# Down matrices 2 to 24 in one 4 MB load each, the last chunks of experts 0 and 1 one by one, and a residual sum moved behind the first up product

## What is computed

```python
x = x + merged @ W_out
h2 = rmsnorm(x, norm_ffn_g)
# per token: the best 4 of 32 router logits, softmax over these four
for e in range(32):                      # rows xb: the tokens that chose e
    gu = xb @ w_gu[e] + b_gu[e]          # (1024, 2048): "up", 8 MB
    g = minimum(gu[:, :1024], 7); lin = clip(gu[:, 1024:], -7, 7)
    y = ((lin + 1) * g * sigmoid(1.702 * g)) @ w_down[e] + b_down[e]   # (1024, 1024): "down", 4 MB
    x[tokens] += weight * y
out = rmsnorm(x, norm_final_g)
```

## Time and profile before

| | us |
|---|---|
| median of 3 runs | 1184.96 (1184.89 to 1185.57) |
| the profiled execution | 1184.24 |
| its span, first to last instruction | 1182.4 |

### The profile page before, as it was taken

One profiled execution on the slowest core, in us unless ns is written; L12 is line 12 of the kernel. 1 busy time (PEld: TensorE's weight loads), 2 busy tenths in 40 slices (PEclk: granted clock), 3 DMA queues, 4 the chain that ended last, 5 costly groups with the idle time before them and its releaser, 6 DMA issues.

```text
span 1182.4 us, 14724 instructions
## 1 busy us (share of the span) xinstructions
PE 1103.6 (93%) x6066; PEld 582.5 (49%) x6066; DVE 391.4 (33%) x647; ACT 247.5 (21%) x389; POOL 4.5 (0%) x10
## 2 busy tenths in 40 slices
PE   8999999999999989898898989898999989998996
PEld 8999999983443333333333333333344333433332
DVE  6768655563222322222222222222222222222212
ACT  6444773432111111111111111111111111111113
POOL 0000000000000000000000000000000000000000
PEclk9999999999999999999999999999999999999999
DMA  9955744689999999999999999999999999999996
GB/s 332 319 175 184 270 164 158 257 318 409 428 425 427 431 431 430 431 427 436 431 430 430 432 432 427 433 430 431 429 432 431 428 432 425 433 428 432 411 422 264
DMA packets 61131, 452.13 MB, mean 382 GB/s; under 512 B 3570, under 2 KB 34535, under 8 KB 40871
## 3 DMA queue, kind: packets, MB, share of 16 engines
q1 hardware_dynamic: 60272, 449.53, 92.0%
q0 software_dynamic: 560, 1.74, 0.5%
q10 hardware_dynamic: 263, 0.34, 0.1%
HBM read 450.53 MB, written 1.06 MB: 382 GB/s over the span
## 4 chain that ended last, share of the span: by engine, by line
DMA 49%; PE 47%; SPq 1%; DVE 1%; ACT 1%; issue 1%; DVEq 0%
DMA dring<-in_w_down_dram 41%; PE bank L1175 17%; PE bank L1546 13%; PE bank L1495 10%; DMA ring<-in_w_gu_dram 7%; PE bank L1440 1%; DMA ring<-in_w_mem_kv_dram 1%; PE bank L1385 1%; PE bank L1266 0%; PE bank L1415 0%; PE bank L1507 0%; PE bank L1449 0%; SPq L315 0%; ACT w_high L487 0%; PE bank L1612 0%
## 5 line engine op out<-in xcount | busy, mean ns | idle before, releaser
L1495 PE MATMUL bank<-ring,region_x 128*64 128x512 f32 x2048 | 456.2, 597 | 6.9 <-DMA ring<-in_w_gu_dram 6.9
L1546 PE MATMUL bank<-dring,region_r 128*64 128x512 f32 x1024 | 247.4, 634 | 56.2 <-DMA dring<-in_w_down_dram 55.7
L1495 PEld LDWEIGHTS bank<-ring,region_x 128*64 128x64 f32 x2048 | 141.0, 137 | 279.7 <-issue 264.8
L1546 PEld LDWEIGHTS bank<-dring,region_r 128*64 128x64 f32 x1024 | 74.4, 145 | 226.2 <-issue 135.0
L1175 PE MATMUL bank<-hT_high,w_high 128*128 128x256 f32 x384 | 109.9, 286 | 0.7 <-DVE hT_low L747 0.7
L1175 PE MATMUL bank<-hT_high,w_low 128*128 128x256 f32 x384 | 108.6, 283 | 0.0
L1175 PE MATMUL bank<-hT_low,w_high 128*128 128x256 f32 x384 | 108.6, 283 | 0.0
L755 DVE TENSOR_TENSOR w_low<-ring,w_high 128x2048 fp32r<-128x2048 f32 x39 | 89.3, 2289 | 52.5 <-ACT w_high L487 52.4
L1083 DVE TENSOR_SCALAR region_r<-bank 128x512 f32<-128x512 f32 x32 | 22.1, 692 | 244.9 <-PE bank L1495 244.9
L1102 DVE SCALAR_TENSOR_TENSOR y_parts<-bank,region_r,y_parts 64x512 fp32r<-64x512 f32 x31 | 23.1, 744 | 215.1 <-ACT y_parts L656 215.1
L639 ACT ACTIVATE region_r<-region_r 128x512 f32<-128x512 f32 x32 | 20.1, 630 | 315.0 <-DVE region_r L1083 315.0
(11 more groups left out here) (248 smaller groups left out, 872.1 us busy)
## 6 DMA issues: line engine op xcount, KB each, us to landing
ring<-in_w_gu_dram SPq DMA_DIRECT2D x50, 4096.0 KB, 25.7
dring<-in_w_down_dram SPq DMA_DIRECT2D x58, 2048.0 KB, 24.2
ring<-in_w_gu_dram SPq DMA_DIRECT2D x17, 2048.0 KB, 12.6
ring<-in_w_in_dram SPq DMA_DIRECT2D x26, 1024.0 KB, 6.4
ring<-in_w_gu_dram SPq DMA_DIRECT2D x22, 1024.0 KB, 8.8
dring<-in_w_down_dram SPq DMA_DIRECT2D x11, 1024.0 KB, 11.6
ring<-in_w_out_dram SPq DMA_DIRECT2D x4, 1024.0 KB, 4.9
ring<-in_w_mem_kv_dram SPq DMA_DIRECT2D x3, 1024.0 KB, 11.8
```

Source lines behind the costliest of these rows:

```text
L1495: last = mm(ps[64 * half:64 * half + 64, :], xg[u // 2][:, c, 64 * (u % 2):64 * (u % 2) + 64], ring[:, slot0 + c, k * F + half * 512:k * F ...
L1546: last = mm(ps[64 * half:64 * half + 64, :], lhsT, dring[:, c // 2, at:at + 512], start=(c == 0), stop=(c == KC - 1))
```

## The change

Six things are changed.

1. `down_slots` reads the matrix as `(p k) n` with k = 8: each partition holds eight neighbouring rows, and n slots of it are one run of n x 8 KB. The runs of loads of every expert stand in two tables, `UP_RUNS` and `DOWN_RUNS`. Down matrices 2 to 24 are one load of 4 MB; before, they were two of 2 MB. Matrices 1 and 25 to 29 stay in two loads, 0, 30 and 31 in four (the last slot of 31 in two). SyncE waits for all slots that a load fills.
2. `down` waits once, at c = 0, for a matrix that comes in one load.
3. The hidden values must stand in the order of the rows: VectorE's reordering goes by eight where it went by four, and four transposes of 128 x 128 become 16 products of 64 x 64 blocks with a piece of the identity.
4. In the small products the slots are transposed first, then the hidden values.
5. Chunks 6 and 7 of experts 0 and 1 are four loads of 1 MB: chunk 6 of both experts after mixer piece 38 of 40, chunk 7 of both after piece 39. Before, they were two loads of 2 MB, both after piece 39.
6. `start_sum(1, 0)` stands behind the first up product.

TensorE's program unrolls four more experts (24 to 27) and its loop runs one turn less; the loop's body is four experts in both.

```diff
+SINGLES = tuple((c, 1) for c in range(KC))
+PAIRS = tuple((c, 2) for c in range(0, KC, 2))
+UP_RUNS = {0: PAIRS[:3] + SINGLES[6:], 1: PAIRS[:3] + SINGLES[6:], 2: SINGLES, 3: SINGLES,
+           4: SINGLES[:4] + PAIRS[2:], E - 2: PAIRS, E - 1: PAIRS[:3] + SINGLES[6:]}
+DOWN_RUNS = {0: SINGLES[:4], 1: PAIRS[:2], E - 2: SINGLES[:4], E - 1: SINGLES[:4]}
+DOWN_RUNS.update({e: PAIRS[:2] for e in range(E - 7, E - 2)})
+def up_runs(e):
+    return UP_RUNS.get(e, ((0, 4), (4, 4)))
+def down_runs(e):
+    return DOWN_RUNS.get(e, ((0, 4),))
+def up_landed(e, c):
+    return sum((c in dict(up_runs(x))) for x in range(e % 2, e + 1, 2))
+def down_landed(e, j):
+    return sum((j in dict(down_runs(x))) for x in range(e + 1))
...
-    hid_fours = hid.rearrange(in_fours, k=4)
-    sg_fours = sg.rearrange(in_fours, k=4)
-    hid_by_row = g_sb.rearrange("p (k q) -> p k q", k=4)
+    in_eights = "p (q k) -> p k q"
+    hid_eights = hid.rearrange(in_eights, k=KC)
+    sg_eights = sg.rearrange(in_eights, k=KC)
+    hid_by_row = g_sb.rearrange("p (k q) -> p k q", k=KC)
...
         def down_slots(expert, j, n):
-            m, k = j // 2, j % 2
             sp.dma_start(dring[:, j:j + n, :].rearrange("p k n -> p (k n)"),
-                         a["w_down"][0, bass.ds(expert, 1), m * 512:(m + 1) * 512, :]
-                         .rearrange("e (p k) n -> p (e k n)", k=4)[:, k * PIECE:(k + n) * PIECE]).then_inc(down_in[j], 16)
-        def expert_down(expert, uses, n=2):
-            for j in range(0, DRING, n):
+                         a["w_down"][0, bass.ds(expert, 1), :, :]
+                         .rearrange("e (p k) n -> p (e k n)", k=KC)[:, j * PIECE:(j + n) * PIECE]).then_inc(down_in[j], 16)
+        def expert_down(expert, uses, runs):
+            for j, n in runs:
                 sp.wait_ge(downs_used, uses + j + n - 1)
                 down_slots(expert, j, n)
...
-        for c in range(0, KC, 2):
-            sp.wait_ge(pieces_used, N_MIX - MIX_RING + 1 + c)
-            up_chunks(1, c, c, 2)
+        for c, n in up_runs(1):
+            sp.wait_ge(pieces_used, N_MIX - MIX_RING + c + n - 1)
+            if c > 5:
+                up_chunks(0, 8 + c, c, n)
+            up_chunks(1, c, c, n)
             if c == 2:
                 down_slots(0, 0, 1)
                 down_slots(0, 1, 1)
-        up_chunks(0, 14, 6, 2)
         sp.wait_ge(pieces_used, N_MIX)
         up_chunks(0, 12, 4, 2)
         down_slots(0, 3, 1)
...
+        expert_down(1, 1, down_runs(1))
+        expert_up(4, 8, N_MIX + 2 * KC + 1, up_runs(4))
+        expert_down(2, 5, down_runs(2))
+        expert_up(5, 0, N_MIX + 3 * KC + 1, up_runs(5))
+        expert_down(3, 9, down_runs(3))
+        whole_up, whole_down = ((0, 4), (4, 4)), ((0, 4),)
         with sp.Fori(0, more * (E // 2) + (E // 2 - 8)) as i:
-            expert_up((i * 2 + 6) % E, 8, i * 16 + (N_MIX - RING + 49))
-            expert_down((i * 2 + 4) % E, i * 8 + 13)
-            expert_up((i * 2 + 7) % E, 0, i * 16 + (N_MIX - RING + 57))
-            expert_down((i * 2 + 5) % E, i * 8 + 17)
+            expert_up((i * 2 + 6) % E, 8, i * 16 + (N_MIX + 4 * KC + 1), whole_up)
+            expert_down((i * 2 + 4) % E, i * 8 + 13, whole_down)
+            expert_up((i * 2 + 7) % E, 0, i * 16 + (N_MIX + 5 * KC + 1), whole_up)
+            expert_down((i * 2 + 5) % E, i * 8 + 17, whole_down)
...
+        def late_down(expert):
+            expert_down(expert, downs + expert * DRING, down_runs(expert))
         for expert in range(E - 10, E - 5):
             half_up(expert, 0)
-            expert_down(expert - 2, downs + (expert - 2) * DRING)
+            late_down(expert - 2)
             half_up(expert, 1)
-        expert_down(E - 7, downs + (E - 7) * DRING)
+        late_down(E - 7)
         for expert in range(E - 5, E - 2):
...
-            dve.tensor_tensor(hid_by_row, hid_fours, sg_fours, ALU.mult).then_inc(hid_ready, 1)
+            dve.tensor_tensor(hid_by_row, hid_eights, sg_eights, ALU.mult).then_inc(hid_ready, 1)
...
         gather_quarter(0)
-        start_sum(1, 0)
...
-        def up(i, u, last_one, between, first=False):
+        def up(i, u, e, between, first=False):
...
-                if (u > 1 and c % 2) or (u == 0 and not first and c in (1, 3)):
-                    pe.wait_ge(piece_in[slot0 + c], 16 * (loads_before(slot0 + c) + 1 + (u == 0)))
                 if c % 4 == 0:
                     pe.wait_ge(piece_in[slot0 + c], i * 32 + 16 * (u // 2) + 16 * (loads_before(slot0 + c) + 1))
-                elif c % 2 == 0:
-                    pairs = 1 + u // 2 + last_one * (2 - u % 2) + 2 * (u == 0 and not first)
-                    pe.wait_ge(piece_in[slot0 + c], 16 * (loads_before(slot0 + c) + pairs))
-                if u == 3 and last_one and c == KC - 1:
-                    pe.wait_ge(piece_in[slot0 + c], 16 * (loads_before(slot0 + c) + 2))
+                elif e is not None and c in dict(up_runs(e)):
+                    pe.wait_ge(piece_in[slot0 + c], 16 * (loads_before(slot0 + c) + up_landed(e, c)))
                 for k, ps in enumerate((gate_ps, lin_ps)):
                     for half in range(2):
...
-        def hidden_transposed(s, halves):
-            pe.wait_ge(hid_ready, s + 1)
-            pe.wait_ge(xg_sb, s + halves)
-            for c in range(4):
-                last = transpose(tr_ps[:, c * P:(c + 1) * P], g_sb[:, c * P:(c + 1) * P], ident)
+        def hidden_transposed():
+            for c in range(KC):
+                for m in range(2):
+                    half = slice(64 * m, 64 * m + 64)
+                    last = mm(tr_ps[half, 64 * c:64 * c + 64], g_sb[half, 64 * c:64 * c + 64], ident[half, half],
+                              start=True, stop=True)
             last.then_inc(hidT_done, 1)
...
         def small_products(i, u, halves=3):
             s = i * 4 + u
-            hidden_transposed(s, halves)
+            pe.wait_ge(hid_ready, s + 1)
+            pe.wait_ge(xg_sb, s + halves)
             pe.wait_ge(y_ready, s + 1)
             slots_transposed(s, y_ps)
+            hidden_transposed()
             scatter_of(s - 1, (u + 1) % 2)
...
             for c in range(KC):
-                if c % 4 == 0:
+                if c % KC == 0:
                     pe.wait_ge(down_in[c // 2], (s + 1) * 16)
-                elif c % 2 == 0:
-                    pe.wait_ge(down_in[c // 2], 16 + 16 * single)
-                lhsT = hidT[:, (c % 4) * P + 64 * (c // 4):(c % 4) * P + 64 * (c // 4) + 64]
+                elif c % 2 == 0 and e is not None and c // 2 in dict(down_runs(e)):
+                    pe.wait_ge(down_in[c // 2], 16 * down_landed(e, c // 2))
+                lhsT = hidT[:, 64 * c:64 * c + 64]
                 for half in range(2):
                     at = (c % 2) * D + half * 512
                     last = mm(ps[64 * half:64 * half + 64, :], lhsT, dring[:, c // 2, at:at + 512],
                               start=(c == 0), stop=(c == KC - 1))
...
-        up(0, 0, False, {0: second_quarter, 2: third_quarter, 3: lambda: gather_quarter(3)}, True)
+        up(0, 0, 0, {0: second_quarter, 2: third_quarter, 3: lambda: gather_quarter(3)}, True)
+        start_sum(1, 0)
...
-        with pe.Fori(0, more * (E // 4) + (E // 4 - 2)) as i:
+        with pe.Fori(0, more * (E // 4) + (E // 4 - 3)) as i:
             for u in range(4):
-                one_expert(i + 1, u)
+                one_expert(i + 1, u, None)
+        for g in range(E // 4 - 2, E // 4 - 1):
+            for u in range(4):
+                one_expert(more * (E // 4) + g, u, 4 * g + u)
```

More of the change, by code:

```diff
@@ L354, in _, with expert_up @@
         sp.dma_start(x_again, a["x"][0].rearrange("(t p) d -> p t d", p=P)).then_inc(x_again_in, 16)
-        def expert_up(expert, slot0, uses, n=4):
-            for c in range(0, KC, n):
+        def expert_up(expert, slot0, uses, runs):
+            for c, n in runs:
                 sp.wait_ge(pieces_used, uses + c + n - 1)
@@ L422, in _ @@
             half_up(expert, 1)
-            expert_down(expert - 1, downs + (expert - 1) * DRING)
-        expert_up(E - 2, 8, ups + (E - 2) * KC, 2)
+            late_down(expert - 1)
+        expert_up(E - 2, 8, ups + (E - 2) * KC, up_runs(E - 2))
         sp.wait_ge(pieces_used, more * (KC * E) + (KC * (E - 2) + N_MIX))
         sp.dma_start(b_down, a["b_down"][0]).then_inc(b_down_in, 16)
-        expert_down(E - 3, downs + (E - 3) * DRING)
-        for c, n in ((0, 2), (2, 2), (4, 2), (6, 1), (7, 1)):
-            sp.wait_ge(pieces_used, ups + (E - 1) * KC + c + n - 1)
-            up_chunks(E - 1, c, c, n)
-        expert_down(E - 2, downs + (E - 2) * DRING, 1)
+        late_down(E - 3)
+        expert_up(E - 1, 0, ups + (E - 1) * KC, up_runs(E - 1))
+        late_down(E - 2)
         for j in range(DRING - 1):
@@ L435, in _ @@
         sp.wait_ge(downs_used, downs + (E - 1) * DRING + (DRING - 1))
[L436 to L438 removed]
+        last_rows = a["w_down"][0, E - 1, :, :].rearrange("(p k) n -> p k n", k=KC)
```

(25 more changed lines are left out.)

26 lines of the change are left out of this document (7 added, 19 removed).

## The result

The changed kernel takes 1187.89 us (median of 9 runs, 1187.12 to 1189.49), the kernel before 1184.89 beside it (9 runs, 1184.32 to 1185.85): a ratio of 1.0027, 95% interval 1.0019 to 1.0036. It is 3.0 us slower, where 1.0 us faster was forecast, and it lies outside the range. Its profiled span is 1185.3 us, 2.9 more than before, so that the two traces show all of the difference.

A forecast was written before the change was run, and what follows sets the result against it. The weight stream was taken to bound the kernel from about 390 us, then TensorE's tail. Terms -1.8 - 1.4 + 1.1 + 0.7 + 0.4 = -1.0 us gave 1184.0 us, with an 8-in-10 range of 1181.3 to 1187.3.

The forecast's parts named there:

- What bounds the kernel: From about 390 us the weight stream sets the end; the tail after its last pieces is TensorE's.
- The start: Closed hole at 254 to 258 and moved residual sum keep 1.35 + 0.5 us of lead: -1.8 us.
- matrix 2: Near the start, its whole load is issued early enough for the stream, by 0.3 us: cost 0.
- The price of the products: 64 x 64 transposes: 32 instructions at 47 ns, +0.9 us an expert, hidden in TensorE's spare time where the stream bounds.
- The tail: After matrix 30's last piece lands, TensorE's slower transposes are not hidden: +1.1 us, from +0.5 to +3.2.
- Rival B: Small products cost 111 ns each, matrix 2 lands 3.8 us late, tail 3.2: +4.9 us, 1189.9; chance 0.12.
- Matrix 20: Little queued ahead of its whole load; even chance of a slow product ahead: +0.7 us, range 0 to 3.5.
- Whole loads in the long stretch: Down matrices 2 to 24 in one load: 23 loads fewer, 0.06 us a matrix, 1.4 us gained, from 0 to 3.
- More code: Unrolled experts and extra instructions: some 7 more instruction blocks loaded over DMA, +0.4 us, from 0 to 2.
- Rival C: The loop of four experts outgrows TensorE's instruction store and is read again each pass: 8 us, 1192; chance 0.04.
- Rival A: At the start all 4.2 us of the stream's lead stays: -3.4 us in sum, 1181.6; chance 0.20.
- Rival D: Each load costs 2.4 us dead time even in a full queue: 55 us less, 1130; chance 0.01.

The follow-up runs named there:

- one_load_only: Kernel before with down matrices 2 to 24 each in one load, old layout and transposes, experts 24 to 27 unrolled; 1187.45 us against 1184.58, ratio 1.0019.
- pairs_20: Changed kernel with down matrix 20 back in two 2 MB loads, experts 20 to 27 unrolled; 1187.42 us against 1185.16 for the kernel before, ratio 1.0019.
- unroll_only: Kernel before with only experts 24 to 27 also unrolled for TensorE, loop one turn shorter; 1185.31 us against 1184.79, ratio 1.0004.
- extra_products: Kernel before with six more 128 x 128 transposes in each expert's small products; 1187.02 us against 1184.79, ratio 1.0020.
- twice_extra: Kernel before with twelve more 128 x 128 transposes in each expert's small products; 1189.74 us against 1185.16, ratio 1.0037.

## Why the prediction was wrong

**What bounds the kernel** was right: the stream from 390 us on, TensorE ahead of it, TensorE's tail. All losses are holes in the stream or steps of the tail.

**The start was the first wrong step** (-1.8 forecast). I read from the least queued load, 6.2 us, that 1.35 us of lead could be kept. The four loads at that place now took 5.3 to 7.3 us, and still nothing of the lead was left at 300. The step treated a queue as full as long as a load takes longer than a lone one. The start is paced by TensorE's releases; the experiments give 0 for the chunks and 0 for the sum.

**Matrix 5 was missed altogether** (put at nothing, without a sum), **and here and in the tail lies what the changed layout cost.** I tested matrix 2 against its issue, found that it fits, and it did (issued 344.05, landed with the stream). For the next load I did not do this sum, though its row stood in the same view: issued at 354.0, landed 13.9 later, 1.8 us more than a lone 12.1. Three experts with +0.86 each less 0.45 make 2.1 us, so even my own price says that this load runs dry, by 0.3 to 0.4; it measured 1.2 in the changed kernel. By the packets, 0.4 of this is the dry queue, as that sum says, and 0.8 the instruction load that fell on one engine just then. The price of the products, which I took for hidden in the stretch bound by the stream, is not hidden in the first four experts.

**The price of the products itself was good.** 32 instructions took 1.08 to 1.10 us, 34 ns each, below the 47 taken and inside the bounds of 28 and 111. Behind them the scatter takes 1.13 instead of 0.93 us and the slots 0.37 instead of 0.22, which the sum had not; together 0.5 + 0.2 + 0.15 = 0.85 an expert against 0.9 forecast. Rows of the chain, one expert of the changed kernel:

```profile
896.32 0.37 PE bank L1535 x2
896.70 1.08 PE bank L1527 x32
897.77 1.13 PE bank L1411 x4
```

The tail followed: +0.9, forecast +1.1. Rival B, 111 ns, is refuted, but its mechanism (late releases open a hole near the start) was the true one at a third of its price, one load further on.

**Matrix 20** got +0.7, in the range 0 to 3.5, for the chance of a product at the slower clock. The product ran at the full clock, and the load still came 1.3 us late. From the chain of the changed kernel:

```profile
835.15 20.37 DMA dring<-in_w_down_dram
...
855.57 7.09 PE bank L1569 x32
```

Issue was at L + 7.2 us, 0.2 behind the forecast's 7.0 (L is the landing of matrix 19). What failed is the 12.1 us of a lone 4 MB load: it took 13.6. In `one_load_only` and the two runs with extra transposes, 12.2 to 12.4. The Trainium skill (DMA: Bandwidth & Descriptors, Anatomy of one DMA) has a fit for loads that GpSimd issues; taken for this load of SyncE, it would give an estimate of 2.0 + 9.6 = 11.6 us; the measured loads are all above that. Why it took 13.6 here and 12.2 in the old layout isn't shown beyond the two late engines; no instruction load is near.

**Matrix 25** had no term of its own, only the +0.4 for more code: it came 1.5 us late, by an instruction load on the engine that was last. A slow product stood ahead of it (8.78 us at 992.95, as the earlier trace rows; the granted clock from 993 to 997 was 0.57, most of it at the lower level), but `pairs_20` has the same and no delay.

**Whole loads in the long stretch**: -0.06 us a matrix forecast, -0.07 measured, right, and only for single runs of 32 KB. **More code**: +0.4 forecast in a range to 2; 8 instruction loads more (7 forecast), of about 1.07 us each (1.35 was taken); `unroll_only` costs 0.5 +/- 1.1 by time. So their size as a mean is not contradicted, but in the changed kernel's trace two of them cost 0.8 and 1.5 us. **Rival C** is refuted: no instruction load in the loop. **Rival A** is refuted by the start. **Rival D** is refuted, whole loads save 0.07 us, not 2.4.

**The sum, redone with measured terms:** start 0 (was -1.8), matrix 5 +1.2 (was 0; 0.4 of it the nearly dry queue), whole loads -1.4 (same), matrix 20 +1.3 (was +0.7), matrix 25 and other delays by instruction loads +0.4 to +1.5 (was +0.4), tail +0.9 (was +1.1): +2.4 to +3.5; measured +3.0. Two terms make up 3.0 of the miss of 4.0: a lead that could not be kept, and a load beside the one that I tested. The parts alone don't add up as neatly: whole loads +2.9, blocks +3.2, chunks +0.9, sum 0, each +/- 1.1 us. That is 7.0 together, against 3.0. The 1.4 us of gain needs both the layout and the whole loads, so no part alone has it. The parts share no edit. The rest, some 2.6 us, is little more than what four such errors make together (2.2), and no run divides it further.

## What to carry to other kernels

Where a producer's releases pace a stream, sum up release, issue and landing for every load until the queue is full, not for the one that looks tightest, and look at the engines one by one: the first of the 16 is through 2 us and more before the load lands. A load that comes too late for them also leaves them level, and then an instruction load on any of them is seen. Moving a stream's start forward gives nothing until something later waits for it and its slots are free; compare the bytes carried by a fixed time. A small extra on an engine that is idle 4 us an expert is free only in the experts in which it is idle.

## What was not expected of the hardware

- A 4 MB load into a nearly dry queue took 12.2 to 12.4 us in three kernels with the old layout; 2.4 us of dead time and 9.7 of bytes make 12.1. In the changed kernel it took 13.3 and 13.6, and 13.4 to 13.5 in three more with blocks; an instruction load has its part in all of these but the 13.6.
- The 16 DMA engines ended their parts of one load 2 us and more apart in a full queue (2.1 at matrix 2 before, 4.1 at matrix 24 in `pairs_20`), and 0.7 to 0.8 us apart where the queue had run dry and no instruction load fell (`extra_products`, `twice_extra`, `one_load_only`).
- In a full queue 4 MB land 9.71 us apart as one run of 32 KB for each partition, 9.79 as two runs of 16 KB, in one load or in two.
- Fp32 products of 64 x 64 blocks went at 34 ns an instruction, where those of 128 columns take 111 and the four transposes of 128 x 128 took 0.60 us.
